# Gate and up panels of the feed-forward stages loaded ahead into homes of their own, with the first block's weight sums, copies and evictions moved

## The reference

```python
def _rmsnorm(x, g):
    xf = x.astype(jnp.float32)
    y = xf * lax.rsqrt(jnp.mean(xf * xf, axis=-1, keepdims=True) + EPS)
    return (y * g.astype(jnp.float32)).astype(x.dtype)

def _swiglu(h, w_gu, w_down):
    g, u = jnp.split(h @ w_gu, 2, axis=-1)
    return (jax.nn.silu(g) * u) @ w_down
...
        x = x + FFN_RES * _swiglu(_rmsnorm(x, norm_ffn1[l]), w_ffn1_gu[l], w_ffn1_down[l])
```

## Time and profile before

| | |
|---|---|
| median of 3 executions | 3335.58 us |
| profiled execution: time | 3338.5 us |
| profiled execution: span, first to last instruction | 3336.4 us |
| PE busy | 3248.6 us (97%) |
| DVE, POOL busy | 1818.1 us, 1803.1 us (54% each) |
| ACT busy | 1131.2 us (34%) |
| mean granted clock of PE | 0.993 of full speed |
| mean DMA rate | 63 GB/s |
| feed-forward stage 1 and 2, first product at | 1128.8 us, 2676.9 us |

### The profile page before, as it was taken

One profiled execution on the slowest core, in us unless ns is written; L12 is line 12 of the kernel. 1 busy time (PEld: TensorE's weight loads), 2 busy tenths in 40 slices (PEclk: granted clock), 3 DMA queues, 4 the chain that ended last, 5 costly groups with the idle time before them and its releaser, 6 DMA issues.

```text
span 3336.4 us, 47997 instructions
## 1 busy us (share of the span) xinstructions
PE 3248.6 (97%) x19068; PEld 1655.5 (50%) x19068; DVE 1818.1 (54%) x2813; ACT 1131.2 (34%) x2104; POOL 1803.1 (54%) x1352
## 2 busy tenths in 40 slices
PE   8999998999999799999999999999999999999999
PEld 4555653655565344444445545555545444444444
DVE  4365558236545887775113376665666687676100
ACT  1434422233341523231002455555555342323000
POOL 4555752446675277674333465555665438777332
PEclk9999999999999999999999999999999999999999
DMA  3112112112021211112222111111112121111312
GB/s 133 41 49 62 59 61 90 53 40 77 26 89 39 82 56 58 64 51 98 71 67 93 32 53 53 56 48 52 36 53 90 47 101 53 62 64 38 109 52 79
DMA packets 59275, 211.70 MB, mean 63 GB/s; under 512 B 7344, under 2 KB 7728, under 8 KB 58544
## 3 DMA queue, kind: packets, MB, share of 16 engines
q1 hardware_dynamic: 54304, 191.34, 17.6%
q10 hardware_dynamic: 4752, 17.30, 1.3%
HBM read 181.36 MB, written 20.97 MB: 61 GB/s over the span
## 4 chain that ended last, share of the span: by engine, by line
PE 94%; DVE 3%; issue 1%; ACT 1%; POOL 1%; DMA 0%; DVEq 0%; POOLq 0%; ACTq 0%
PE pair L1184 27%; PE pair L1185 26%; PE pair L1186 26%; PE pair L1404 3%; PE pair L1373 3%; PE pair L1385 2%; PE pair L1622 1%; PE pair L1648 1%; PE pair L1633 1%; PE pair L1576 1%; PE pair L1204 1%; DVE arena L2155 1%; PE pair L1362 0%; POOL panel_parts L967 0%; ACT residual L1905 0%
## 5 line engine op out<-in xcount | busy, mean ns | idle before, releaser
L1184 PE MATMUL pair<-operand,panel_parts 128*128 128x512 f16 x1808 | 693.2, 383 | 47.8 <-DVE operand L2155 26.1
L966 POOL TENSOR_SCALAR panel_parts<-panel_raw 128x1024 f16<-128x1024 f32 (+3 forms) x204 | 209.0, 1024 | 920.7 <-issue 654.4
L1185 PE MATMUL pair<-operand,panel_parts 128*128 128x512 bf16 x1808 | 690.6, 382 | 0.0
L1186 PE MATMUL pair<-operand,panel_parts 128*128 128x512 f16 x1808 | 690.4, 382 | 0.0
L1184 PE MATMUL pair<-arena,panel_parts 128*128 128x512 f16 (+1 forms) x1248 | 471.3, 378 | 8.9 <-issue 4.4
L967 POOL TENSOR_TENSOR panel_parts<-panel_raw,panel_parts 128x1024 bf16<-128x1024 f32 (+3 forms) x204 | 469.2, 2300 | 17.0
L1003 POOL TENSOR_SCALAR arena<-arena,row_inv 128x256 f32<-128x256 f32 (+7 forms) x256 | 344.6, 1358 | 236.4 <-DVE row_inv L2221 236.1
L1185 PE MATMUL pair<-arena,panel_parts 128*128 128x512 bf16 (+1 forms) x1248 | 470.5, 377 | 0.0
L1186 PE MATMUL pair<-arena,panel_parts 128*128 128x512 f16 (+1 forms) x1248 | 470.3, 377 | 0.0
L1184 PEld LDWEIGHTS pair<-operand,panel_parts 128*128 128x128 f16 x1808 | 177.5, 98 | 283.1 <-issue 94.8
L2158 DVE SCALAR_TENSOR_TENSOR residual<-pair,residual 128x1024 f32<-128x1024 f32 (+1 forms) x64 | 61.3, 958 | 420.0 <-PE pair L1186 392.1
(11 more groups left out here) (300 smaller groups left out, 5979.1 us busy)
## 6 DMA issues: line engine op xcount, KB each, us to landing
panel_raw<-in_wl SPq DMA_DIRECT2D x58, 512.0 KB, 3.5
panel_raw<-in_wm SPq DMA_DIRECT2D x56, 512.0 KB, 3.6
ffn_extra<-in_wgu SPq DMA_DIRECT2D x18, 1024.0 KB, 5.0
panel_raw<-in_wgu SPq DMA_DIRECT2D x18, 1024.0 KB, 5.1
panel_raw<-in_wdn SPq DMA_DIRECT2D x32, 512.0 KB, 3.5
residual<-residual_spill SPq DMA_DIRECT2D x31, 512.0 KB, 6.9
residual_spill<-residual ACTq DMA_DIRECT2D x24, 512.0 KB, 2.6
panel_raw<-in_wgu SPq DMA_DIRECT2D x16, 512.0 KB, 3.6
```

Of the source, the lines that this page charges most:

```text
L966: chained(nc.gpsimd.tensor_scalar(hi[:, c], RAW[:, s, c], HI_MAX, -HI_MAX, ALU.min, ALU.max))
L1184: nc.tensor.matmul(out, stat[0], mov[0], start=first, stop=False, skip_group_check=skip)
L1185: nc.tensor.matmul(out, stat[0], mov[1], start=False, stop=False, skip_group_check=skip)
L1186: return nc.tensor.matmul(out, stat[1], mov[0], start=False, stop=last, skip_group_check=skip)
```

## The change

Panels gu(0,0) and gu(0,1) of both stages leave the ring. One SP load fetches both into `ffn_extra`: for stage 1 in layer 2, after the second group of residual tiles and ahead of output panel o3; for stage 2 in turn 2 of the mixer, ahead of the bias table. POOL splits them at the place where it split them before, into the columns of `ffn_extra` that later hold block 0's first four weight slots, counts them on a semaphore of their own, and PE takes them from there. The ring carries gu(0,2) and gu(0,3) instead, both split without a wait for a product. Block 0's raw load follows the load of gu(0,3) and waits for the early split alone. The squares move from `ffn_extra` to the arena. On ACT, weight copy 0 moves ahead of the term copies, and the copy of term T4 ahead of weight copies 5 and 6. On POOL, T4's rest moves ahead of weight rests 5 and 6. On DVE, block 0's four weight sums move ahead of plain pair 1, eviction 0 of block 0 ahead of the tail of pair 3, and evictions 1 and 2 of block 0 ahead of block 1's weight sums.

```diff
-PANEL_SECTIONS = [("layers", 1, len(LPANELS)), ("gu1", PLAIN_F // 2, 4), ("down1", 2, 12),
-                  ("mix", 1, len(MIX_PANELS)), ("out", 1, 1), ("gu2", PLAIN_F // 2, 4), ("down2", 2, 12)]
+PANEL_SECTIONS = [("layers", 1, len(LPANELS)), ("gu1a", 1, 2), ("gu1", PLAIN_F // 2 - 1, 4), ("down1", 2, 12),
+                  ("mix", 1, len(MIX_PANELS)), ("out", 1, 1), ("gu2a", 1, 2), ("gu2", PLAIN_F // 2 - 1, 4), ("down2", 2, 12)]
...
+def gu_panel(idx, i, j):
+
+    return (f"gu{idx}a", 0, j - 2) if i == 0 else (f"gu{idx}", i - 1, j)
...
-        SQT = [arena(c, 1024) for c in (11264, 12288, 26624, 27648, 22528, 24576)] + [EXR[:, 0:1024], EXR[:, 1024:2048]]
+        SQT = [arena(8192 + 1024 * k, 1024) for k in range(KT)]
...
-        THIRD_FFN = {1: parts(18432, 1024), 2: parts(17280, 1024)}
+        EARLY = [slot_parts_of(EX[:, 2048 + 1024 * n:3072 + 1024 * n]) for n in range(2)]
...
+            def early_panels(idx):
+                sp.dma_start(EXR.rearrange("p (j c) -> p j c", j=2), io[f"wgu{idx}"][0, 0:2].rearrange("j p c -> p j c")).then_inc(early_loaded, 16)
...
                 residual_back(l, (2, 3, 6, 7))
+                if l == LAYERS - 1:
+                    early_panels(1)
...
             def ffn(idx):
-                for i in range(PLAIN_F // 2):
-                    for j in range(4):
-                        panel(f"gu{idx}", i, j, io[f"wgu{idx}"][i, j])
-                for b in range(BLOCKS):
...
-                    if b == 0:
-                        sp.wait_ge(square_added, 7 * idx)
...
+                for i in range(PLAIN_F // 2):
+                    for j in range(2 if i == 0 else 0, 4):
+                        panel(*gu_panel(idx, i, j), io[f"wgu{idx}"][i, j])
+                    if i == 0:
+                        sp.wait_ge(early_split, 2 * idx)
+                        raw(0)
+                for b in range(1, BLOCKS):
...
                     sp.wait_ge(mix_max, 2 * TT * j)
+                if j == 2:
+                    early_panels(2)
...
                 restart()
-                for j in range(2):
-                    panel(f"gu{idx}", 0, j, 1024, None)
-                panel(f"gu{idx}", 0, 2, 1024, (gate_r_made, 2 * MIX_TURNS) if idx == 2 else None, THIRD_FFN[idx])
-                panel(f"gu{idx}", 0, 3, 1024, tile_done(f"gu{idx}", 0, 1))
+                pool.wait_ge(early_loaded, 16 * idx)
+                for n in range(2):
+                    raw, (hi, lo) = EXR[:, 1024 * n:1024 * (n + 1)], EARLY[n]
+                    chained(nc.gpsimd.tensor_scalar(hi, raw, HI_MAX, -HI_MAX, ALU.min, ALU.max))
+                    nc.gpsimd.tensor_tensor(lo, raw, hi, ALU.subtract).then_inc(early_split, 1)
+                for j in (2, 3):
+                    panel(*gu_panel(idx, 0, j), 1024, None)
...
                 term_rest(B_T2, Q22, 0)
-                for i in range(7):
+                for i in range(5):
                     weight_rest(0, i)
                 term_rest(B_T4, Q21, 1)
+                for i in range(5, 7):
+                    weight_rest(0, i)
...
+                def gu_weights(i, j):
+                    if i == 0 and j < 2:
+                        pe.wait_ge(early_split, 2 * (idx - 1) + j + 1)
+                        return EARLY[j]
+                    return weights(*gu_panel(idx, i, j))
...
+                    elif b == 0 and i < 4:
+                        j = i // 2
+                        act.wait_ge(tile_ready[j], tiles_before(f"gu{idx}", 0, j) + 1)
                     copy(WSLOT[q % NSLOTS][0], weight_source(b, i)).then_inc(weight_hi, 1)
...
                 plain_silu(0)
+                weight_part(0, 0)
                 for home, q, n in ((B_T1, Q11, 9), (B_T3, Q12, 10), (B_T2, Q22, 11)):
                     term_part(home, q, n)
                 plain_silu(1)
-                for i in range(5):
+                for i in range(1, 5):
                     weight_part(0, i)
                 for f in range(2, PLAIN_F):
                     plain_silu(f)
+                act.wait_ge(tile_ready[3], tiles_before(f"gu{idx}", PLAIN_F // 2, 3))
+                term_part(B_T4, Q21, 12)
                 for i in range(5, 7):
                     weight_part(0, i)
-                act.wait_ge(tile_ready[3], tiles_before(f"gu{idx}", PLAIN_F // 2, 3))
-                term_part(B_T4, Q21, 12)
...
-                plain_pair(1)
                 for n in range(4):
                     weight_sum(0, n)
+                plain_pair(1)
                 term_clip(B_T2, 3).then_inc(term_clipped, 1)
                 term_split(B_T1, Q11, 1)
                 plain_pair(2)
                 term_split(B_T3, Q12, 2)
-                plain_pair(3)
+                plain_front(3)
                 term_clip(B_T4, 4).then_inc(term_clipped, 1)
+                evict(0, 0)
+                plain_back(3)
                 for b in range(BLOCKS):
                     more = b + 1 < BLOCKS
                     if b > 0:
                         keep_block(b - 1)
-                    evict(b, 0)
+                    if b > 0:
+                        evict(b, 0)
+                    else:
+                        evict(b, 1)
+                        evict(b, 2)
                     if more:
                         for n in range(4):
                             weight_sum(b + 1, n)
-                    evict(b, 1)
-                    evict(b, 2)
+                    if b > 0:
+                        evict(b, 1)
+                        evict(b, 2)
```

More of the change, by code:

```diff
@@ L478, in build, with slot_parts_of @@
         Q11, Q12, Q21, Q22 = (X4[:, k:k + 4, c:c + HALF] for k in (0, 4) for c in (0, HALF))
+        def slot_parts_of(v):
+            return v.bitcast(HI)[:, 0:1024], v.bitcast(LO)[:, 1024:2048]
         def slot_parts(v):
@@ L589, in build @@
         ffn_spilled = sem("ffn_spilled")
+        early_loaded = sem("early_panels_loaded")
+        early_split = sem("early_panels_split")
         raw_loaded = [sem(f"raw_loaded{n}") for n in range(2)]
@@ L882, in ffn @@
                     sp.dma_start(dst, src).then_inc(raw_loaded[b % 2], 16)
+                for i in range(PLAIN_F // 2):
[5 more added lines that the diff above has]
+                for b in range(1, BLOCKS):
+                    if b == 1:
+                        for j in (2, 3):
+                            sp.wait_ge(panel_split[panel_slot(f"gu{idx}", j)], panels_before(f"gu{idx}", PLAIN_F // 2 - 2, j) + 2)
+                    else:
+                        sp.wait_ge(weight_lo, 7 * block_of(idx, b - 1))
+                    raw(b)
                 sp.wait_ge(weight_lo, 7 * BLOCKS * idx)
@@ L1058, in ffn @@
                         else:
-                            used = turn_before(f"gu{idx}", i, j + 2)
-                        panel(f"gu{idx}", i, j, 1024, used)
+                            used = tile_done(f"gu{idx}", 0, j + 2) if i == 1 else turn_before(f"gu{idx}", i, j + 2)
+                        panel(*gu_panel(idx, i, j), 1024, used)
                 def weight_rest(b, i):
@@ L1478, in ffn, with gu @@
             def ffn(idx, xbase, before=None):
-                def gu(i, j, home=None):
+                def gu_weights(i, j):
[3 more added lines that the diff above has]
+                    return weights(*gu_panel(idx, i, j))
+                def gu(i, j):
                     dst = acquire(f"gu{idx}", i, j)
-                    w = weights(f"gu{idx}", i, j)
-                    w = home or w
+                    w = gu_weights(i, j)
                     for c in (0, HALF):
@@ L1489, in ffn @@
                 dsts = [acquire(f"gu{idx}", 0, j) for j in range(2)]
-                ws = [weights(f"gu{idx}", 0, j) for j in range(2)]
+                ws = [gu_weights(0, j) for j in range(2)]
                 for k in range(KT):
@@ L2568, in plain_pair, with plain_front @@
                 def plain_pair(f):
+                    plain_front(f)
+                    plain_back(f)
+                def plain_front(f):
                     i, j = divmod(f, 2)
```

11 lines of the change are left out of this document (5 added, 6 removed).

## The result

Over ten runs of each kernel the change takes 1.0023 of the time before, 95% interval 1.0015 to 1.0030: medians 3348.43 against 3340.64 us, +7.8 us, within the 0.3% that the prediction called no change. The forecast was +7.6 us. It was put at 3343.2 us because the three runs then known of the kernel before had their median at 3335.58; seven more raised it by 5 us, so the sum is to be held against the ratio; the 3348.43 itself lies within the stated 3326 to 3350, near its upper end. The profiled execution has a span of 3344.7 us against 3336.4, +8.3.

A forecast was written before the change was run, and what follows sets the result against it. PE's matrix work, 94% of the chain of waits, was taken as the bound. Terms +2.1 + 0.5 + 2.5 + 2.5 = +7.6 us on the median 3335.58 gave 3343.2 us, range 3326 to 3350.

The forecast's parts named there:

- Fetching early: Both stages: loading two panels early costs 0 and gains 0, since POOL still passes the same wait before splitting them.
- Stage 1's start: First operand of stage 1: four panel splits in a row take turns with DVE's operand chain, +2.1 us, no gain possible.
- Stage 2's start: Start of stage 2: two more splits beside DVE make the second operand late, +0.5 us; the 3.28 us wait stays.
- steps 1 to 5: Stage 1, block 0: moved sums and turned T2/T1 order delay DVE; fourth product waits 2.5 us instead of 0.52.
- Step 6: Block 0's sixth product: evictions 1 and 2 end at 1238.0, a 2.9 us wait, 1.1 us later than before.
- Step 7: Block 1's fourth product: block 1's sums and evictions come late, a new wait of about 1.4 us.
- the last two alone: Middle: the two eviction moves on DVE, without the sums' move, would nearly end block 0's 3.65 us wait.
- The clock, price 0: Middle: the 2.9 us gap most likely still drops PE to clock 0.50, so that cost stays, 0 change.
- twice 2.5: Middles of both stages: 1.1 + 1.4 = +2.5 us in stage 1, and the same in stage 2.
- (a): Rival, DVE on time: sums and splits do not hold each other; −6.9 us, 3328.7, at best 3324.0; chance 0.25.
- (b): Rival, products 3 to 6 of block 0: the 2.5 us wait also drops the clock; +11.6 us, 3347.2; chance 0.25.
- (c): Rival, nothing moves: waits change places within 2 us a stage, only starts show; 0 to +4 us, 3338; chance 0.15.

The follow-up runs named there:

- middle back: Changed kernel with DVE, ACT and POOL in their old middle order (except ACT's weight copy 0); early panels, homes and early load kept; 1.0006 of the kernel before.
- split in the mixer: Changed kernel with POOL splitting the early panels at the end of layer 2 (stage 1) and in the mixer's turn 4 (stage 2); 1.0016 of the kernel before.
- panel 3 late: Changed kernel with the split of panel 3 again waiting for the product of panel 1; 1.0015 of the kernel before.
- split ahead: Changed kernel with POOL splitting the early panels before its wait for the end of the layers (stage 1) and mixer (stage 2); 1.0033 of the kernel before.
- Sums back: Changed kernel with block 0's four weight sums again behind the second plain pair; 0.9992 of the kernel before.
- T1 first: Changed kernel with DVE's clip and subtraction for term T1 put ahead of its clip for T2, sums still early; 1.0011 of the kernel before.
- sums early and evictions first: Changed kernel with evictions first in all 18 blocks, block 0's weight sums still ahead of the second plain pair; 0.9993 of the kernel before.
- all blocks and the mixer split: Changed kernel with sums back, evictions first in all 18 blocks, early panels split at layer 2's end and in mixer turn 4; 0.9943 of the kernel before, 3323.92 us.
- middle alone: Kernel before, without early panels, with eviction 0 and T4 moved ahead and evictions first in all 18 blocks; 0.9951 of the kernel before, 3322.44 us.

## Why the prediction was right

- **Fetching early, cost 0 and gain 0:** right. Stage 2 still waits 3.19 us for POOL, middle back waits 3.22, and the table shows no panel wait. The reason given, that POOL passes the same wait first, is half of it: split in the mixer shows that without POOL's wait PE waits 3.33 us for DVE's first operand, and the start gets no shorter.
- **Stage 1's start, +2.1:** measured +1.9, and panel 3 late takes away 2.5, so its cause is shown. What the sum left out is small: the clock came back 0.7 us sooner and operand waits added 0.6. That no gain is possible there was wrong: with the split out of DVE's way the wait is 11.28 us in split ahead, 1.8 less than before.
- **Stage 2's start, +0.5:** waits for the first operand, 0.87, and the second, 0.46, came where 0.5 at the second was worked out, but the clock did not fall behind 3.19 us as it had behind 3.28, which gave 1.1 back. Up to the fourth panel the start cost 0.2 net, 50.4 us for 50.2.
- **The middle, steps 1 to 5:** the changed trace is 0.75 us later from the fourth panel on, so on the clock of before pair 1 starts at 1194.3 (1194.4 was worked out), pair 2 at 1211.0 (1211.1), the last pair at 1223.5 (1223.4), and the wait is 2.53 (2.5). Sums back and T1 first show both causes: with either undone the fourth product of block 0 does not wait.
- **Step 6:** 2.9 was worked out, 2.81 came in stage 1. In stage 2 the clock fell behind the fourth product's 2.52 already, PE wanted the sixth later, and it waited 1.12.
- **Step 7, the new wait of 1.4 at block 1's fourth product:** the step that failed, in place and size. In stage 1 it is 1.60 at the *sixth*; in stage 2 it is 0.87 at the fourth and 2.37 at the sixth. I counted block 1's sums and evictions, but not that block 2's sums stand ahead of eviction 1 of block 1 and wait there for POOL's rests. And I counted PE's five products up to block 1's fourth at 2.6 us each, 13.0 in sum, although the working itself had the clock at 0.50 behind the 2.9 us wait. In stage 1 the clock did fall, and they took 14.63 us (1238.90 to 1253.53), so that eviction 0 of block 1, done at 1252.63 + 0.68 = 1253.31, was in time and no wait came. In stage 2, where the clock stayed at 1.00 behind the sixth product, they took 13.1 us and the wait of 0.87 came. The omission of block 2's sums also made too much of the evictions: the 3.65 us wait does nearly end (0.44 in sums back, where eviction 0 and T4 are moved as well, so for "the last two alone" it is not shown), but the gain is passed on as a wait in block 1.
- **The clock, price 0:** right in stage 1, where it fell once in both. In stage 2 it fell behind 2.52 and 2.37, 1.7 us each, in place of the start's 1.1 and the middle's 2.5. The two stages together are +3.1 (from 0.76 us late ahead of block 0 to 3.87 behind block 1) and +3.9, for twice 2.5.
- **What made up for it:** −1.2 us in the layers. That is within what executions differ by there: the last output product of layer 2 starts at 1103.19 us in the run with sums early and evictions first and at 1110.10 in sums back, which have the same layers. Without it the profiled execution would have been 9.5 us longer than the one before. So that +7.6 met the measured +7.8 so closely is partly luck: two middles that cost 2.0 us more than forecast were set off by these 1.2 us and by starts that cost 0.5 less.
- **Rivals:** (a) fell, as DVE was not on time. (b), a second slow stretch, came in stage 2 alone, in two blocks (0 and 1) and not within block 0. (c) fell, the middle carries 7 of the 8.3 us.

## What to carry to other kernels

An instruction that is moved to fill an idle engine is paid for by what the neighbour engine does in that moment: ask of each new place what the other engine runs there and whether the moved operands are in SBUF or PSUM. When a wait is taken out of a repeated block, look in the next block for the same instruction order, since the lateness goes on to it; the order has to be right in all of them. An early load pays only if the work behind it, here the split, is early too, lies where the other engine has no deadline, and is what the stage waits for: in stage 2 DVE's operand was as late as the panels.

## What the runs showed of the hardware

The length of a wait alone does not tell whether PE's clock falls. Windows of the changed kernel (columns as in the earlier trace rows):

```profile
1231.00:1233.00 2.00, 2.00 (x11) 0.94 (x10) 2.00 (x1) 0.00 (x0) 2.00 (x1) 1.00 0.00 0
...
1241.00:1243.00 2.00, 2.00 (x7) 0.71 (x6) 2.00 (x2) 1.58 (x4) 1.92 (x3) 0.53 1.01 408
2679.00:2681.00 2.00, 1.13 (x6) 0.32 (x5) 2.00 (x2) 0.38 (x1) 1.92 (x2) 1.00 0.77 236
2786.00:2788.00 2.00, 2.00 (x6) 0.76 (x5) 2.00 (x1) 0.00 (x0) 2.00 (x2) 0.50 0.00 0
```

Behind 2.53 us of waiting the clock stayed at 1.00, behind 2.81 us in the same block it fell, and behind 2.52 us at the place of the 2.53 in the other stage it fell to 0.50; behind 3.19 us it stayed. (0.50 is 1.2 GHz.) In the run with sums early and evictions first the same wait of 3.19 us at the same place was followed by 0.50:

```profile
2672.00:2674.00 2.00, 2.00 (x6) 0.60 (x5) 1.93 (x1) 0.56 (x1) 1.92 (x2) 0.50 0.68 168
```

What decides it is open. The prediction's rule, that waits of somewhat over 2 us drop it, was read from too few rows.

The blocks run in one of two rhythms, in one and the same kernel. PE in 200 us of either stage, kernel before:

```profile
1300.00:1500.00 200.00, 199.38 (x917) 88.73 (x916) 147.91 (x175) 61.65 (x110) 140.99 (x153) 1.00 0.18 59
2850.00:3050.00 200.00, 200.00 (x929) 90.48 (x927) 137.30 (x177) 61.63 (x110) 150.01 (x156) 1.00 0.18 58
```

In stage 1 it starts 917 matrix instructions where stage 2 starts 929, at clock 1.00: at the fourth product of each block one start comes 0.44 us behind the last instead of 0.22, which falls below what the timeline marks as idle. Fifteen such steps are 3.3 us a stage. The profiled execution of sums back has it in neither stage, middle back in both. That part of the spread of the kernel before (3335.28 to 3343.95 us in ten runs) comes from it is argued, not shown, since one execution of each is profiled. With the evictions first in all blocks (all blocks and the mixer split, middle alone) neither stage has it.
